# VectorE's order in a latent attention: the former item's scaling ahead of the next item's maximum, and other slots for a small Hyena mixer

## The reference

```python
def mla_attention(q_nope, q_rope, k_nope, k_rope, v):      # 8 heads, blocks of 128 queries
    s = (einsum('bqhd,bkhd->bhqk', qn, k_nope) + einsum('bqhr,bkr->bhqk', qr, k_rope))
    prob = softmax(s * scale, axis=-1)
    return einsum('bhqk,bkhd->bqhd', prob, v)

def hyena_mix(u, ...):
    u = short_conv(u, conv_w, conv_b)
    x0, x1, v = split(u, 3)
    z = x1 * v
    y = irfft(rfft(z, 2 * L) * rfft(k, 2 * L))[:L] + d_bias * z
    return x0 * y
```

## Time and profile before

| | us |
|---|---|
| median of 3 runs | 3452.97 |
| the profiled execution, its own time | 3458.23 |
| its span | 3456.4 |
| PE busy | 3291.2 (95%) |
| DVE busy | 1999.9 (58%) |
| ACT busy | 1312.4 (38%) |
| first layer's attention | about 293 to 480 of the span |
| second layer's attention | about 1234 to 1373 of the span |

### The profile page before, as it was taken

One profiled execution on the slowest core, in us unless ns is written; L12 is line 12 of the kernel. 1 busy time (PEld: TensorE's weight loads), 2 busy tenths in 40 slices (PEclk: granted clock), 3 DMA queues, 4 the chain that ended last, 5 costly groups with the idle time before them and its releaser, 6 DMA issues.

```text
span 3456.4 us, 42703 instructions
## 1 busy us (share of the span) xinstructions
PE 3291.2 (95%) x17650; PEld 2718.3 (79%) x17650; DVE 1999.9 (58%) x2797; ACT 1312.4 (38%) x1949; POOL 56.7 (2%) x59
## 2 busy tenths in 40 slices
PE   7898999999999999999989999999899999899998
PEld 3685568888888755988887888888888888788887
DVE  6677676777556476565557655333654564563333
ACT  3323455232234245533354445222533333362223
POOL 0000000000000000000000010000100000020000
PEclk8899999999999999999999999999999999999999
DMA  5541022545443320355522212332233333223221
GB/s 177 169 129 66 13 80 91 159 153 158 154 153 125 95 68 25 119 190 183 178 71 77 78 62 86 109 99 91 58 94 80 73 86 80 65 83 101 98 98 49
DMA packets 375408, 356.13 MB, mean 103 GB/s; under 512 B 73471, under 2 KB 320558, under 8 KB 373807
## 3 DMA queue, kind: packets, MB, share of 16 engines
q1 hardware_dynamic: 374995, 353.32, 33.4%
q10 hardware_dynamic: 220, 0.07, 0.0%
HBM read 345.50 MB, written 4.72 MB: 101 GB/s over the span
## 4 chain that ended last, share of the span: by engine, by line
PE 51%; DVE 5%; ACT 3%; issue 1%; POOL 0%; DMA 0%; SPq 0%; DVEq 0%; ACTq 0%; POOLq 0%
PE ps L414 45%; PE ps L2819 1%; DVE r_st L2702 1%; PE ps L2840 1%; ACT second_scr L734 1%; DVE second_w_lo L582 1%; PE ps L2829 1%; DVE x_res L918 1%; ACT second_w_hi L522 0%; DVE second_scr L916 0%; PE ps L2842 0%; DVE sums L498 0%; DVE second_scr L745 0%; PE ps L2548 0%; PE ps L2554 0%
## 5 line engine op out<-in xcount | busy, mean ns | idle before, releaser
L414 PE MATMUL ps<-second_h_hi,second_w_hi 128*128 128x512 f32 (+1 forms) x2216 | 819.6, 370 | 45.2 <-DVE second_h_lo L944 24.3
L414 PE MATMUL ps<-second_h_hi,second_w_lo 128*128 128x512 f32 (+1 forms) x2216 | 806.5, 364 | 0.0
L414 PE MATMUL ps<-second_h_lo,second_w_hi 128*128 128x512 f32 (+1 forms) x2216 | 805.5, 364 | 0.0
L582 DVE TENSOR_TENSOR second_w_lo<-ring,second_w_hi 128x2048 fp32r<-128x2048 f32 (+2 forms) x175 | 371.5, 2123 | 454.1 <-ACT second_w_hi L522 454.1
L414 PEld LDWEIGHTS ps<-second_h_hi,second_w_hi 128*128 128x128 f32 x2216 | 424.8, 192 | 112.1 <-issue 27.8
L414 PEld LDWEIGHTS ps<-second_h_hi,second_w_lo 128*128 128x128 f32 x2216 | 424.1, 191 | 65.0
L414 PEld LDWEIGHTS ps<-second_h_lo,second_w_hi 128*128 128x128 f32 x2216 | 424.7, 192 | 60.9
L522 ACT ACTIVATE second_w_hi<-ring 128x2048 fp32r<-128x2048 f32 (+2 forms) x175 | 309.8, 1770 | 272.9 <-PE ps L414 264.1
L414 PE MATMUL ps<-h_mix_hi,w_mix_hi 128*128 128x512 f32 (+2 forms) x776 | 268.9, 346 | 8.3 <-DVE w_mix_lo L582 4.3
L414 PE MATMUL ps<-h_mix_lo,w_mix_hi 128*128 128x512 f32 (+2 forms) x776 | 266.4, 343 | 0.0
L414 PE MATMUL ps<-h_mix_hi,w_mix_lo 128*128 128x512 f32 (+2 forms) x776 | 266.2, 343 | 0.0
(11 more groups left out here) (476 smaller groups left out, 5401.1 us busy)
## 6 DMA issues: line engine op xcount, KB each, us to landing
ring<-in_w_mlp SPq DMA_DIRECT2D x64, 1024.0 KB, 5.4
side_w<-in_ada_w SPq DMA_DIRECT2D x96, 512.0 KB, 4.9
ring<-in_ffn_w_in SPq DMA_DIRECT2D x44, 1024.0 KB, 5.0
side_w<-in_w_mod SPq DMA_DIRECT2D x80, 512.0 KB, 3.8
ring<-in_attn_w_in SPq DMA_DIRECT2D x48, 512.0 KB, 5.3
ring<-in_hgrn_w_in SPq DMA_DIRECT2D x32, 512.0 KB, 4.9
ring<-in_ffn_w_out SPq DMA_DIRECT2D x16, 1024.0 KB, 5.1
ring<-in_w_in SPq DMA_DIRECT2D x14, 1024.0 KB, 5.5
```

Source lines behind the costliest of these rows:

```text
L414: mm = pe.matmul(acc, lhsT, rhs, start=at == 0 and wp == ap, stop=at == j.kt - 1 and wp == 1)
L582: dve.tensor_tensor(unit.place(unit.slot[1]), unit.place(M.ring[:, u % RING, :]), unit.place(unit.slot[0]), ALU.subtract).then_inc(*S.w_lo ...
```

## The change

It does two things, and both alter nothing but the order of instructions on DVE. PE's, ACT's, POOL's and SP's lists stay the same, instruction for instruction. No instruction is added or removed.

```diff
     def vector(self, dve):
         for n in range(self.n_items + 4):
             yield self.at(n, 2.6)
+            if 1 <= n <= self.n_items:
+                self.normalise(dve, n - 1)
             if n < self.n_items:
                 self.maximum(dve, n)
-            if 1 <= n <= self.n_items:
-                self.normalise(dve, n - 1)
             if n >= 4 and n % 2 == 0:
                 yield self.at(n, 5)
                 self.store(dve, n // 2 - 2)
...
-            hc = HyenaThread(X, some, LX, LC, (fill(9), fill(9, 1)), [fill(u, 4.5) for u in range(2, 8)], fill(10), [fill(11), fill(11, 1.7)],
-                             [fill(13), fill(13, 1.7)], hx)
+            hc = HyenaThread(X, some, LX, LC, (fill(9), fill(9, 1)), [fill(u, -1.2) for u in range(2, 8)], fill(10), [fill(11), fill(11, 4.0)],
+                             [fill(13), fill(13, 4.0)], hx)
```

## The result

The changed kernel takes 3458.93 us (median of 20 runs, 3453.96 to 3464.44) against 3453.59 us before (20 runs, 3449.82 to 3461.48). The ratio is 1.0013, with a 95% interval from 1.0007 to 1.0019: slower by some 5 us, and within the 0.3% that I took as "no change". Runs of one kernel scatter by 4 to 8 us to either side of their median. For the whole time I therefore go by medians, and use the traces for where it went.

What follows compares the result with a forecast made beforehand. PE bounds the kernel, busy 3291.2 of 3456.4 us. First layer to item 38 -3, its last ten items +3, second layer +1.6: +1.6 on the profiled 3458.23, less 5.3 to reach the median, gives 3454.5 us; range 3443 to 3464.

Steps and rivals of the forecast that it cites:

- What the swap removes: First layer's attention up to item 38: transposes' waits for a late scaling shrink or vanish, about -5 us.
- late exponents and stores: First layer before item 38: delays of a few tenths each, together another 2 us added.
- three more places: First layer: first head projection +0.5 us, last one +1.1, values waiting for the context's first mix +0.6.
- The moved convolutions, mix and ending: Context's side work on DVE: counted within the removed waits; if cover is gone, up to 1.7 us at three or four places.
- The clock: First layer, behind the 1.88 us stall: L2002 and six transposes regain speed, 1.2 + 0.5 = 1.7 us won.
- the projection that I left at 5.49 us: First layer's slow head projection, against 2.84 us elsewhere: stays as it is, with the gap of about 2.2 us around it.
- The last ten items: End of the first layer's attention: no projections left, so the maximum, exponent, scaling chain rules, +3 us.
- The second layer: Second layer's attention: nothing to win from 1255 to 1350, small delays at start and end, together +1.6 us.
- The other signs: First layer's trace: L1921 waits 15 us or more for L1882, maxima start behind scalings, scores wait in items 41 to 47.
- my two signs for being wrong: First layer's attention shorter by over 6 us, or scores waiting for exponents in the middle of a layer.
- The chain: Rival, chance 0.10: maximum, exponent and scaling set the pace in both layers, up to 0.75 us per wide unit, some +12: 3465.
- The third rival: Chance 0.05: small new stalls across PE's list lower the clock at three or four more places, +8 to +11, so 3464.

Runs made afterwards that it cites:

- the blocks alone: Kernel before with only the context's six convolutions, second mix and second ending moved, maximum still before scaling: 3445.03 us, ratio 0.9975.
- the swap alone: Kernel before with only the scaling put ahead of the maximum in both layers, convolutions, mix and ending unmoved: 3468.20 us, ratio 1.0038.

## Why the prediction was right, and where it wasn't

**The total.** I forecast 3454 us, in the range 3443 to 3464, and no change within 0.3%. The time is 3458.93. My sum said +1.6 us and the medians say +5.3. Behind that stand two large effects in opposite directions, -8.4 and +13.9 us, and my sum has neither at its size. That together they came so near my number was luck.

**What the swap removes (-5 us up to item 38).** The waits went, as forecast: 1.1 us of transposes' waits for L1923 are left, and I had said under 4. The blocks take part in that: alone they leave 6.5 of 10.0 us. The step that failed is the balance. I gave late exponents and stores 2 us together, and 1.1, 0.6 and 0.5 us to three more places. The runs show that the swap costs 4.7 us in the middle where I had it at about -1 (-5 + 0.5 + 1.1 + 0.6 + 2). In their place stand PE's waits for stores (+2.8, with L2002 that waits 0.9 us twice and that my walk missed) and for ACT's copies (+1.1), and a lower clock behind them (2.6 us), for which my sum had nothing. Of the three places none came as priced in the changed kernel: the first head projection waits 0.15 us more than before, the last 0.40 less, and the values behind the context's mix 0.2 us in both.

**The moved convolutions, mix and ending.** I counted them as part of the removed waits. This is the largest error: they had a price of their own, -8.4 us by medians and -10.4 in the trace's middle, and I gave them none. I wrote that at the end of a unit a convolution delays the next maximum and scaling, which was the right mechanism. Its 1.7 us for six convolutions, 10 us, was the number to set beside the measured 11.7.

**The clock (-1.7 us).** The term was mis-sized. L2002 went from 3.09 to 2.00 us, as forecast (334.09 us in the trace after), but the projection that I left at 5.49 us takes 4.54 in the changed kernel and 2.84 with the blocks alone. The reason I gave, "the gap of about 2.2 us around it stays", doesn't hold: with the blocks alone the stall ahead of the gap is gone. Nor did the whole term arise where I put it: before, the clock was lower at the first projection too (4.27 us at 316.21), which takes 2.84 us after the change.

**The last ten items (+3 us).** Measured +5.1, of which 1.5 are idle time of PE and 3.6 clock. The sign and the waits for exponents were right, but the term was mis-sized on both counts: the chain itself is half of what I gave it, and the clock I left out. The timeline of the changed kernel shows the forecast signs, scores that wait for exponents and then matmuls at a lower clock:

```profile
456.75 1.56 PE L1823 MATMUL ps<-mx_k,mx_q 96*128 96x512 f32 x4 [0.57 <-ACT f L1882]
...
460.21 1.56 PE L1823 MATMUL ps<-mx_k,mx_q 96*128 96x512 f32 x4 [0.40 <-ACT f L1882]
...
462.96 0.70 PE L1823 MATMUL ps<-mx_k,mx_q 96*128 96x256 f32 x2 [0.53 <-ACT f L1882]
...
465.02 0.99 PE L1837 MATMUL ps<-ident,f 128*128 128x128 f32 x6 [1.36 <-ACT mx_probs L1874]
...
465.94 2.83 PE L1851 MATMUL ps<-mx_probs,mx_v 128*64 128x256 f32 x12
...
476.28 0.63 PE L414 MATMUL ps<-h_mix_lo,w_mix_hi 128*128 128x512 f32 x1
...
479.73 0.39 PE L414 MATMUL ps<-h_mix_lo,w_mix_hi 128*128 128x512 f32 x1
```

The values L1851 take 2.83 us where other groups of twelve take 1.51, and the projection's L414 take 0.63 us each until 479 instead of 0.39. Before, the tail's clock was 1.00 throughout.

Of the 3.6 us of clock 1.6 can't be laid to the swap. With the convolutions moved alone, with none, and with the swap in the middle alone, PE's idle times from item 38 to the output projection are those of before, one by one, and yet L414 starts at the lower clock. With the convolutions moved alone:

```profile
470.33 0.63 PE L414 MATMUL ps<-h_mix_lo,w_mix_hi 128*128 128x512 f32 x1
```

In all three the projection's first 24 matmuls take 1.6 us more than before.

**The second layer (+1.6 us).** Measured +0.8 in the changed kernel and +0.9 with the swap in that layer alone. The sign was right, the size double. The values end 0.8 us later where I had said 1.5, and PE is busy 93.8 us between 1255 and 1350, against 94.4 before.

**The other signs.** L1921 waits 8.6 us for exponents, where I said 15 or more. What DVE does between (rope, mix, low parts) may cover the rest; I didn't measure that. Of the 80 maxima 78 stand behind a scaling and 69 start at its end, as said. The first head projection waits 1.14 us against 0.98 before, where I had said 0.5 more, and its store frees the bank late enough for 2.31 us when the convolutions stay in their old place. The tail's scores wait for exponents in three items, as said. Of my two signs for being wrong neither came: the middle gained 5.7 us, under the 6 that I had named for the whole attention, and no scores wait for exponents there. They were signs of the sum, and could not tell a small gain of the swap from a large one of the blocks less a loss of the swap.

**The rivals.** The chain (0.10) is the nearest to what happened. In its pure form, +0.75 us for each wide unit, it is wrong: the second layer's full windows lose nothing. Its price of +12 is near the +13.9 and +14.8 that the swap costs, but it was reckoned for the whole change and by another way, so that is no confirmation. The third rival, more short gaps and a lower clock behind them, is part of it: of the 9.8 us that the swap adds to the blocks in the first layer 6.2 are clock (2.6 + 3.6), with 1.6 of them in doubt as said. The Trainium skill, "TensorE: Matmul & The Clock Gate", section "A second HAM failure mode: psum-queue depth-cycling", describes a kernel in which frequent short idles between groups of matmuls make the clock swing. The traces agree in kind: in the first layer's attention no wait of PE is over 1.9 us before or 1.8 after, and the clock falls in both. That more short waits are worse than a few long ones was my own inference. The total idle time doesn't decide it either: with the swap at even items PE idles 11.4 us in the middle at a clock of 1.00, in the changed kernel 11.3 at 0.99, which is 2.4 us more of PE's busy time.

**What stays open.** Outside the attentions, where no kernel differs, traces still part by several microseconds. From the first layer's output projection to the second layer's scores, the kernel before and then the swap alone:

```profile
485.80:1234.10 748.30, 734.66 (x4105) 634.62 (x4104) 485.51 (x708) 250.64 (x352) 1.78 (x3) 1.00 0.45 141
494.40:1248.40 754.00, 740.28 (x4106) 638.58 (x4105) 485.15 (x708) 250.44 (x352) 3.30 (x3) 0.99 0.44 139
```

The swap alone takes 5.6 us longer there, the changed kernel 2.8 and the blocks alone 2.5. PE's idle time is 13.4 to 13.9 us in all four, so the difference is the granted clock. Behind the second layer's attention it goes the other way: before is 3.6 us longer than the swap alone and 1.0 longer than the changed kernel. I didn't run enough profiles to say whether the edits cause it or executions differ so anyway. Such shifts may hold part of the 14.8 us of the swap alone, of which the trace places 4.1 + 5.3 + 0.9 = 10.3 us in the two attentions. What sets the clock is open too. In idle time alone, which repeats from trace to trace, the swap costs PE 2.1 us in the middle, 1.5 in the tail and 0.8 in the second layer: 4.4 of its 13.9 us.

**The best version** is the one with the blocks alone: 3445.03 us, 0.25% faster than before and, by the two medians, 0.4% faster than the changed kernel. It keeps the maximum ahead of the scaling.

## What to carry to other kernels

When a change has two parts, price each by itself, and ask for a sign that tells them apart. A sum near nothing says nothing of its terms. In a loop that two engines share, put the operation that feeds the other engine (here the maximum, which starts ACT's exponential) ahead of the one that only finishes the item before (the scaling), unless PE waits longer for the latter than the former may slip (no run here tested such a case). Put side work of 1 or 2 us on a half idle engine where that engine waits anyway, not ahead of the step that feeds the others: six convolutions of 1.7 us cost 10 to 12 us in one place and 3 to 5 in the other, by medians and by trace.

## What the runs showed of the hardware that was not expected

The same six projection matmuls behind the same idle of 0.99 us take 5.49 us at 347.34 and 2.84 us at 402.97 of one trace, and with the blocks alone 2.84 us at the first of these places. 2.84 us is the clock's upper level of 2.4 GHz, and 5.49 nearly all at 1.2 GHz. In the slow case a stall of 1.20 us ends 1.4 us before the projection starts. Of the 10.4 us that the blocks win in the middle of the first layer 6.4 are clock. So short idles close together can be dearer than their sum. But it is no fixed price: behind a gap of 1.72 us the same matmuls take 4.54 us in the changed kernel and 2.84 with the swap at even items, and with the same idle times ahead of it the output projection of the first layer runs at the upper clock in three traces (before, the blocks alone, the swap in the second layer) and 1.6 us slower in three others.

What repeats is the course of PE's idle times: in the traces of two kernels that are the same up to there, the first layer's middle takes 154.9 and 154.9 us, and 149.1 and 149.2. Whole executions of one kernel differ by up to 0.3% (3449.82 to 3461.48 us for the kernel before), so one profile of each kernel can hide a difference of 5 us, as it did here.
